# Attention inside a decoder step on one core: the value product's operands swap places, and head rows are transposed on TensorE instead of moved by DMA

## What is computed

```python
# q: 8 heads of 64; keys and values: 2 groups; T = 1024 tokens in blocks of 128
p_c = masked_softmax(q . kc, valid_c)          # 32 compressed keys
p_s = masked_softmax(q . ks, kpos <= q_pos)    # selected keys (here all, causal)
p_w = masked_softmax(q . k_win, valid_w)       # window of 512
out = g0 * (p_c @ vc) + g1 * (p_s @ vs) + g2 * (p_w @ v_win)   # (token, head, 64)
y_b = out.reshape(B, T, 512)                   # goes on to "y_b @ w_proj_b"
```

## Time and profile before

| | before |
|---|---|
| median of 3 runs | 2473.39 us (2472.95 to 2475.03) |
| profiled execution, its own time | 2473.83 us |
| its span in the trace | 2472.0 us |
| PE busy | 2288.4 us, 93% |
| DVE busy | 826.4 us, 33% |
| ACT busy | 501.9 us, 20% |
| attention stage (first exponential to last `att_out`) | about 605 to 1083 us of the span |
| merge stage begins | 1082.8 us |

### The profile page before, as it was taken

One profiled execution on the slowest core, in us unless ns is written; L12 is line 12 of the kernel. 1 busy time (PEld: TensorE's weight loads), 2 busy tenths in 40 slices (PEclk: granted clock), 3 DMA queues, 4 the chain that ended last, 5 costly groups with the idle time before them and its releaser, 6 DMA issues.

```text
span 2472.0 us, 30188 instructions
## 1 busy us (share of the span) xinstructions
PE 2288.4 (93%) x11143; PEld 1726.6 (70%) x11143; DVE 826.4 (33%) x1909; ACT 501.9 (20%) x1029; POOL 292.6 (12%) x274
## 2 busy tenths in 40 slices
PE   4979999996888888899999999898999999989998
PEld 1245567775655566566667766678999999978886
DVE  0131123247666666653211111552111111133343
ACT  2020001011333333321111011442111111123232
POOL 0000001101000000003200001530000000035543
PEclk9989999997999999999999999999999999999999
DMA  7620100101200000035341342431111111134553
GB/s 269 224 75 26 43 17 18 35 2 69 78 4 4 4 5 4 4 96 154 113 117 57 100 119 86 161 122 52 51 48 37 51 34 51 34 120 128 179 171 103
DMA packets 179724, 189.40 MB, mean 77 GB/s; under 512 B 10069, under 2 KB 149437, under 8 KB 179198
## 3 DMA queue, kind: packets, MB, share of 16 engines
q1 hardware_dynamic: 178590, 184.12, 23.8%
q10 hardware_dynamic: 1056, 4.23, 0.5%
HBM read 173.88 MB, written 16.53 MB: 77 GB/s over the span
## 4 chain that ended last, share of the span: by engine, by line
PE 77%; DVE 11%; issue 5%; ACT 3%; DMA 3%; DVEq 0%; ACTq 0%; SPq 0%; POOL 0%; PEldq 0%
PE ps L2173 20%; PE ps L2091 14%; PE ps L1774 8%; PE ps L1790 5%; PE ps L2139 4%; PE ps L2140 4%; PE ps L2141 4%; PE ps L1742 3%; PE ps L1968 3%; DVE arena L1368 2%; PE ps L1951 2%; PE ps L1927 1%; DVE arena L1389 1%; ACT arena L902 1%; DMA arena<-in_w_out 1%
## 5 line engine op out<-in xcount | busy, mean ns | idle before, releaser
L2173 PE MATMUL ps<-h_hi,wup_hi 128*128 128x344 f32 x1056 | 340.6, 323 | 18.5 <-PE ps L2173 11.2
L2173 PE MATMUL ps<-h_lo,wup_hi 128*128 128x344 f32 x1056 | 339.3, 321 | 0.0
L2173 PE MATMUL ps<-h_hi,wup_lo 128*128 128x344 f32 x1056 | 339.0, 321 | 0.0
L2139 PE MATMUL ps<-rw_hi,ra_hi 128*128 128x512 f32 x540 | 217.7, 403 | 17.4 <-DVE rw_lo L1550 11.3
L2173 PEld LDWEIGHTS ps<-h_hi,wup_hi 128*128 128x128 f32 x1056 | 199.5, 189 | 24.8 <-issue 24.2
L2140 PE MATMUL ps<-rw_hi,ra_lo 128*128 128x512 f32 x540 | 214.1, 397 | 0.0
L2141 PE MATMUL ps<-rw_lo,ra_hi 128*128 128x512 f32 x540 | 213.5, 395 | 0.0
L2091 PE MATMUL ps<-hT,arena 128*128 128x344 f32 x704 | 211.1, 458 | 0.0
L1774 PE MATMUL ps<-arena,hT 128*128 128x386 f32 (+1 forms) x576 | 190.2, 491 | 12.1 <-DMA arena<-in_w_in 12.1
L2173 PEld LDWEIGHTS ps<-h_lo,wup_hi 128*128 128x128 f32 x1056 | 199.4, 189 | 0.0
L2173 PEld LDWEIGHTS ps<-h_hi,wup_lo 128*128 128x128 f32 x1056 | 199.2, 189 | 0.0
(11 more groups left out here) (380 smaller groups left out, 2733.4 us busy)
## 6 DMA issues: line engine op xcount, KB each, us to landing
hT<-in_w_down SPq DMA_DIRECT2D x66, 512.0 KB, 3.5
arena<-in_w_ada SPq DMA_DIRECT2D x12, 2048.0 KB, 7.9
arena<-in_w_up SPq DMA_DIRECT2D x44, 512.0 KB, 4.9
arena<-in_w_in SPq DMA_DIRECT2D x30, 512.0 KB, 4.8
arena<-in_w_out SPq DMA_DIRECT2D x24, 512.0 KB, 3.6
arena<-in_cache_cmp_kv SPq DMA_DIRECT2D x64, 128.0 KB, 2.0
arena<-in_cache_slc_kv SPq DMA_DIRECT2D x128, 64.0 KB, 1.9
arena<-in_w_in SPq DMA_DIRECT2D x4, 1544.0 KB, 9.0
```

What stands on the lines that cost most here:

```text
L2139: nc.tensor.matmul(out, ra_hi[rnd][a][:, rows], rw_hi[rnd][w][:, cols], start=(k == 0), stop=False)
L2173: ins = nc.tensor.matmul(ps[:, bank, 0:TG], w[:, k0 + k, :], h[:, k, toks], start=(k == 0 and j == 0), stop=(k == KD - 1 and j == 2))
```

## The change

The operands of the value product change places: `ptbuf`, the transposed weights (128 keys by 128 tokens), are stationary, and the values (128 keys by 64) stream. The result has the tokens on the partitions and 64 columns. `att_out` copies 128 by 64 to `ynat[i]`, a tile of token rows that holds all heads side by side (512 columns); two of the eight tiles lie where `ost` was and behind it, six in `Pm`'s columns 1024 to 1535, which the sample stage's page loads write later. The loop on SP with its 8 DMAs goes, and so does ACT's wait for them. After the last head PE transposes the 8 tiles with 4 transposes each, through PSUM banks 0 to 3; DVE evicts the even tiles to `ybT`, ACT the odd ones, and PE waits for the first four evictions before tile 4. SP waits for all 32 transposes (`s_yn`) before it loads what the sample stage needs. Four semaphores of the sample stage are made one; what they order is the same.

```diff
-        ost = take(HD, SEQ)
+        ynat = [take(P, NH * HD) for _ in range(2)] + [Pm[:, i, SEQ:SEQ + NH * HD] for i in range(2, NT)]
...
-            with sp.Fori(0, NH // 2) as j:
-                for odd in range(2):
-                    sp.wait_ge(s_comb, j * 2 * NT + (odd * NT + NT + 1))
-                    sp.dma_start(ybT[odd * HD:(odd + 1) * HD, bass.ds(j, 1), 0:SEQ], ost.unsqueeze(1)).then_inc(s_ybd, 16)
...
+            sp.wait_ge(s_yn, NT)
             sp.dma_start(sC2, flat_rows(t["state_mlstm_C"], DQ * DV)).then_inc(s_wc, 16)
...
             def att_out(i, h):
                 act.wait_ge(s_pv, h * NU + (2 * i + 2))
-                if i == 0:
-                    act.wait_ge(s_ybd, h * 16 + 16)
-                nc.scalar.activation(ost[:, i * P:(i + 1) * P], ps[0:HD, 6 + i % 2, 0:P], ACT.Copy).then_inc(s_comb, 1)
+                nc.scalar.activation(ynat[i][:, bass.ds(h * HD, HD)], ps[:, 6 + i % 2, 0:HD], ACT.Copy).then_inc(s_comb, 1)
...
+            for i in range(1, NT, 2):
+                act.wait_ge(s_yn, i + 1)
+                nc.scalar.activation(ybT[:, :, i * P:(i + 1) * P], ps[:, i % 4, :].rearrange("p (j t) -> p j t", t=P),
+                                     ACT.Copy).then_inc(s_ybd, 1)
...
+            for i in range(0, NT, 2):
+                dve.wait_ge(s_yn, i + 1)
+                nc.vector.tensor_copy(ybT[:, :, i * P:(i + 1) * P], ps[:, i % 4, :].rearrange("p (j t) -> p j t", t=P))                  .then_inc(s_ybd, 1)
...
-                    ins = nc.tensor.matmul(ps[0:HD, 6 + i % 2, 0:P], v, src, start=(kind == "w" and o == 0),
+                    ins = nc.tensor.matmul(ps[:, 6 + i % 2, 0:HD], src, v, start=(kind == "w" and o == 0),
...
             pe.wait_ge(s_comb, NH * NT + 1)
+            for i in range(NT):
+                if i == NT // 2:
+                    pe.wait_ge(s_ybd, NT // 2)
+                for j in range(NH // 2):
+                    ins = nc.tensor.transpose(ps[:, i % 4, j * P:(j + 1) * P], ynat[i][:, j * P:(j + 1) * P], ident)
+                ins.then_inc(s_yn, 1)
...
                 if u == 0:
-                    pe.wait_ge(s_ybd, 16 * (NH + 1))
+                    pe.wait_ge(s_ybd, NT)
```

More of the change, by code:

```diff
@@ L380, in build @@
         s_yb, s_ybd = sem("ybT_sample"), sem("ybT_rows")
+        s_yn = sem("y_rows_T")
         s_scr, s_scrg, s_smp, s_newwin = sem("scratch"), sem("scratch_gates"), sem("sample_in"), sem("new_win")
@@ L384, in build @@
             sem(n) for n in ("pages_used", "pages_weighted", "pages_T", "pages_act", "pages_dve", "q_padded"))
[L385 to L388, removed]
+        s_sps, s_Qall, s_soft, s_softm, s_softe, s_sPT, s_sPTe = (
+            sem(n) for n in ("samples_ps", "Q_all", "soft", "soft_max", "soft_exp", "sPT_ps", "sPT"))
+        s_cg, s_cge, s_sWd, s_sWp, s_sh2, s_shd, s_sCn, s_sya = (
+            sem(n) for n in ("sm_gate", "sm_exp", "sm_W", "sm_W_ps", "sm_h", "sm_std", "sm_C", "sm_ya"))
+        SP_Q, SP_Y, SP_IMP, SP_O = 1, 2, 3, 4
         s_wmg, s_wl = ([sem(f"{n}{j}") for j in range(2)] for n in ("wmerge", "w_up"))
@@ L889, in _ @@
             act.sem_inc(s_comb, 1)
-            act.sem_inc(s_ybd, 16)
             def att_exp(u, h):
@@ L1436, in samples_dve @@
                 if n == 1:
-                    dve.wait_ge(s_Qps, 1)
+                    dve.wait_ge(s_sps, SP_Q)
                     for g in range(NKV):
@@ L1512, in samples_dve @@
                 if n == 22:
-                    dve.wait_ge(s_impps, 1)
+                    dve.wait_ge(s_sps, SP_IMP)
                     step(nc.vector.tensor_reduce(imp, ps[0:SR, 4, 0:NCMP].rearrange("p (k r) -> p k r", r=2), AX.X, ALU.add))
@@ L1539, in samples_dve @@
                 if n == 32:
-                    dve.wait_ge(s_Osum, 1)
+                    dve.wait_ge(s_sps, SP_O)
                     for h in range(NH):
@@ L2004, in samples_pe @@
                         ins = nc.tensor.transpose(ps[:, 5, 64 + j * NS:64 + (j + 1) * NS], Ps[:, lo:lo + P], ident[0:NS, 0:NS])
-                    ins.then_inc(s_Qps, 1)
+                    ins.then_inc(s_sps, 1)
                 if n == 3:
@@ L2031, in samples_pe @@
                         pe.wait_ge(s_sh2, 2)
-                        nc.tensor.transpose(ps[:, 5, 256:288], hv, ident[0:32, 0:32]).then_inc(s_syT, 1)
+                        nc.tensor.transpose(ps[:, 5, 256:288], hv, ident[0:32, 0:32]).then_inc(s_sps, 1)
                     for j in range(NPAGE):
@@ L2041, in samples_pe @@
                     pe.wait_ge(s_soft, 2)
-                    nc.tensor.matmul(ps[0:SR, 4, 0:NCMP], cst("same_group", SR), pcm, start=True, stop=True).then_inc(s_impps, 1)
+                    nc.tensor.matmul(ps[0:SR, 4, 0:NCMP], cst("same_group", SR), pcm, start=True, stop=True).then_inc(s_sps, 1)
                 if n == 24:
@@ L2071, in samples_pe @@
                 if n == 32:
-                    nc.tensor.matmul(ps[:, 0, 0:SR], ones[0:1, :], zrow[:, 0:SR], start=False, stop=True).then_inc(s_Osum, 1)
+                    nc.tensor.matmul(ps[:, 0, 0:SR], ones[0:1, :], zrow[:, 0:SR], start=False, stop=True).then_inc(s_sps, 1)
             def scores(b):
```

4 lines of the change are left out of this document (3 added, 1 removed).

## The result

The changed kernel takes 2481.15 us (median of 8 runs, 2477.04 to 2484.38) against 2473.86 us for the kernel before in the same job (8 runs): a ratio of 1.003, 95% interval 1.0019 to 1.004. That is 7.3 us more, 4.7 to 9.9; the forecast was 6.0. The profiled execution is the slowest of the eight: 2484.38 us, a span of 2482.6 us.

What follows compares the result with a forecast made beforehand. PE was taken to bound the stage behind the attention, DVE and ACT much of each head. 4.56 + 8 x 0.18 = 6.0 us on the profiled 2473.83 gave 2479.8, or 2479.4 for the median; 8-in-10 range 2476.5 to 2486.

Steps and rivals of the forecast that it cites:

- Part 4: After the last head: the 32 transposes delay the merge stage by 4.56 us, 0.9 of it PE's wait; bounds 4.0 to 5.3.
- The first sigmoid: In the merge stage: ACT's preparation ends before the first sigmoid is due, so it stays hidden, by about 1.2 us.
- Part 1: Value product: a pass goes from 0.109 to 0.111 us, the load now setting it; 0.18 us a head lost.
- The ends I take to cancel: At each group of value passes: first load 0.053 us longer, last stream shorter by as much, so no net effect.
- the term of 1.44 us for eight heads: Value passes where PE leads: a loss of 0.18 us a head, counted over 8 heads.
- Part 2: ACT's copy of the result: shorter copy against a new register instruction, taken as 0; bounds -0.06 and +0.06 us a head.
- Part 3: Output DMAs on SP's queue: nothing in the attention waits for them on the path, so removing them gains nothing.
- The stream was the price: Value passes: loads hide, a pass falls from 0.109 toward 0.053 us; 7.3 to 23 us faster; chance 0.06.
- The loads stand open: Value groups: each first load exposed by 0.053 us without a shorter tail; +8.5 to +14.4 us; chance 0.14.
- The clock falls at the end: Merge stage: PE's new wait lowers the clock for as much as 10 us, costing 5 us more; chance 0.08.
- Only the end pays: Whole kernel: value passes cost nothing net, only the end's transposes count; 4.0 to 4.6 us slower; chance 0.24.
- its second form: In the heads: ACT's shorter copy and the shorter last stream give back the passes' cost; total 4.0 to 4.6 us.

Runs made afterwards that it cites:

- e1_no_transposes: The changed kernel without PE's 32 transposes at the end, the transposition left out of the result: 2473.82 us, ratio 1.0001 to the kernel before.
- e2_old_plus_T: The kernel before, DMAs and old product kept, with 32 transposes of other data at the attention's end: 2481.11 us, ratio 1.003.
- e12_half_product: The kernel before with 64 columns streamed through the 64-column stationary values, half the product left out of the result: 2459.66 us, ratio 0.994.
- e5_wide_values: The kernel before with 128 stationary value columns instead of 64, ACT's head loop written twice: 2470.18 us, ratio 0.9985.
- e6_double_stream: The changed kernel with 128 value columns streamed in each pass instead of 64: 2475.76 us, ratio 1.0004 to the kernel before.
- e0_after: The changed kernel run again without any edit: 2481.22 us, ratio 1.003 to the kernel before.
- e7_plain_work: The kernel before with five unread float32 products of 512 columns ahead of the merge stage: 2480.84 us, ratio 1.0026.
- e4_warm: The kernel before with 24 transposes of constants in PE's idle stretch at each head's end: 2473.12 us, ratio 0.9998.

## Why the forecast came out, point by point

**The total** was right: 6.0 us forecast, 7.3 (4.7 to 9.9) measured. It rests on Part 4, and that is shown from both sides: `e1_no_transposes` is level with before, `e2_old_plus_T` has the whole loss. The other 1.4 us of the sum, for the passes, came out near by luck, as below.

**Part 4, the end**, was right in its working: 4.46 us for 4.56, the wait 0.69 for 0.9. The first sigmoid wasn't late: it came 4.83 us behind the merge stage's first pass (4.94 before), with ACT idle for 1.09 us ahead of it, where 1.2 was forecast.

**Part 1, the passes**: that the load of 128 stationary columns holds a pass at 0.111 to 0.112 us was right, at 8, 64 and 128 streamed columns alike. The Trainium skill, page "TensorE: Matmul & The Clock Gate", section "LDWEIGHTS (loading the stationary operand)", puts such a load at 107 ns; the trace has 112. `e12_half_product` shows the other side: with both halved, the pass falls. The step that failed is "The ends I take to cancel". The head ends of four kernels (timelines, one head each, all at a clock of 1.00; the heads of a kernel agree to 0.03 us) take the groups' ends apart, from T(15)'s first pass to the next head's first exponential:

| | stationary, streamed | that way, us | PV(15) up to the next pass, us |
|---|---|---|---|
| before | 64, 128 | 7.01 | 1.89 |
| `e5_wide_values`, a head with table load | 128, 128 | 6.92 | 1.87 |
| `e6_double_stream` | 128, 128 | 7.04 | 1.87 |
| changed | 128, 64 | 6.88 | 1.82 |

The closed gaps give 0.09 us a head (7.01 to 6.92), the thinner stream another 0.16 (7.04 to 6.88), where the forecast had a loss of 0.07 for PV(14) and PV(15). That the heads still came out 0.1 us *longer* each (seven heads 419.1 us in the changed kernel, 419.5 in `e0_after`, 418.4 before; the forecast was 0.18 a head) has two causes. In the middle units shorter groups only lengthen PE's wait for DVE, 12.5 us in all. And on the chain the clock takes it back: at the same clock the changed heads are some 0.2 us shorter, but two of seven, and three in `e0_after`, stand at 0.89 and are 0.6 to 0.8 us longer. So the term of 1.44 us for eight heads was about right (0.7 and 1.1 us over seven heads in two profiles) by luck: it had a price of the passes, where the passes gave something back and the clock, which the sum put at nothing, cost as much and more.

**Part 2, the copy**, was taken as nil, with bounds of 0.06 us a head. It costs 0.12: `e5_wide_values` and `e6_double_stream` have the same passes, and `e6_double_stream`, with the register instruction ahead of its copy, takes 7.04 us for 6.92. ACT's copy begins 2.16 us behind PV(15)'s first pass rather than 2.07, and of the rest the shorter copy takes back all but 0.02. That is 0.9 us over eight heads, hidden in the total by the gain of the groups.

**Part 3, the DMAs**: nil, as far as the noise lets see; `e2_old_plus_T` keeps them and costs the same as the change.

**The rivals.** "The stream was the price" is out: loads are 0.112 us apart. "The loads stand open" is out: groups got shorter. "The clock falls at the end" is out as put: from the transposes to the end of the next stage the granted clock is no lower than before (0.98 for 0.97). The clock did matter, in the heads, where no rival had it. "Only the end pays" is nearest to what `e1_no_transposes` shows, and its second form, that shorter ends of the groups give back what the passes cost, is what the head ends show; its 4.0 to 4.6 us lie just under the interval's lower end.

**What stays open.** The traced stage accounts for 4.9 us (changed kernel) and 5.3 (`e0_after`) of 7.3; in `e2_old_plus_T` 4.1 of 7.3, in `e7_plain_work` 4.4 of 6.4. Three of the four lie inside the timed interval, `e2_old_plus_T`'s 0.8 us below its own (4.9 to 10.1), and all four lie on the same side of the medians. The work behind the attention isn't consistently slower: it takes 1389.2 us before, 1392.9 in the changed kernel's profile and 1385.9 in `e0_after`'s. Single profiles differ there by as much as what is sought, so some 2 us are not located. Nor is it settled which of the two opposite terms in the heads, groups and clock, is the larger in the timed runs.

## What to carry over

Before swapping which operand is stationary, write down both the load's and the stream's time: the pass goes at the slower of the two, so halving the stream gains next to nothing if it doubles the load (the groups' ends alone), and every pass added where PE leads is paid in full. A pass saved where PE waits for another engine becomes waiting, and can cost through the clock. Compare stretches that have the same granted clock, head by head, before laying a difference to the passes. Look at each loop's first instruction on ACT for a table load: one instruction ahead of the loop was worth twice what the whole change cost.

## What the runs showed of the hardware

- **A table load in every trip of a loop.** ACT loaded a table at the start of each head, 1.28 us each. With one exponential ahead of the loop all eight loads are gone, one has come ahead of the stage, and the kernel is 15 us faster. `e5_wide_values`' second loop, which is entered with the exponential's table in place, has none. The Trainium skill, page "ScalarE: Activation LUTs", section "What ACT_TABLE_LOAD costs", gives 1283 ns for the load, as here, and about 1380 ns more for a drain. At the head's end the second part doesn't show: from ACT's copy to the next exponential it is 1.84 us before (843.23 to 845.07) and 0.55 without the load (839.10 to 839.65), 1.29 less. By the page's figures the eight would be 21 us, an estimate; the attention stage became 12.1 us shorter with the seven in it, not all of which need be the loads', and the whole kernel 15, and the measurement decides.
- **Narrow stationary operands open gaps.** Around groups of 64 stationary columns, and where 128 rows change to 32 inside one, PEld's row has gaps of 0.17 us (though none ahead of PV(15), 841.23); with 128 columns they are gone in these places, even at the 32 rows. Over the whole stage the value product's loads stood behind 46.8 us of such idle time in 128 places before, and 10.7 us in 43 after. Why isn't settled.
- **A thinner stream, a lower clock.** With the same loads, at the same pace of 0.112 us, streaming 128 columns (`e6_double_stream`) rather than 64 (the changed kernel) raised the attention's granted clock from 0.90 to 0.92, lowered the time at 1.2 GHz from 198 to 166 us and made the stage 2.3 us shorter, though 64 of the columns are read by nobody and each head end got 0.16 us longer. A head took 59.0 us at a clock of 1.00 (`e4_warm`), 59.1 at 0.97 and 59.7 at 0.91 (before), and in the changed kernel 59.5 at 0.91 and 60.2 at 0.89.
